# Pair sums of the late token chunks in a one-core PEER kernel: 64 candidates in place of 256

## The reference, cut to what matters

```python
s = jnp.einsum('chpd,hpnd->chpn', q, sub_keys)          # two halves p, 128 keys each
st, it = lax.top_k(s, 16)                               # best 16 of each half, in falling order
cand = st[:, :, 0, :, None] + st[:, :, 1, None, :]      # 16 x 16 = 256 pair sums
best, pos = lax.top_k(cand.reshape(...), 16)            # best 16 pairs
eidx = it_0[pos // 16] * 128 + it_1[pos % 16]           # the expert's number, of 16384
g = softmax(best)
act = gelu(u_tab[eidx] . x)                             # rows of 1024 numbers
y = sum((g * act) * v_tab[eidx])                        # rows of 1024 numbers
```

## Time and profile before

| | |
|---|---|
| median of 3 runs | 2634.97 us (2634.31 to 2636.11) |
| the profiled execution's own time | 2656.55 us |
| its span, first to last instruction | 2654.8 us |
| DVE busy | 1962.0 us (74%) |
| PE busy | 1695.6 us (64%) |
| POOL busy | 1067.3 us (40%) |
| ACT busy | 425.3 us (16%) |
| mean DMA rate over the span | 284 GB/s |

### The profile page before, as it was taken

How to read it: one execution, slowest core, us unless ns; L and a number is a source line. 1 busy time by engine, 2 the same in 40 slices (tenths; PEclk the granted TensorE clock), 3 DMA queues, 4 the chain that set the end, 5 groups by cost and what they waited for, 6 DMA issues and landing times.

```text
span 2654.8 us, 19535 instructions
## 1 busy us (share of the span) xinstructions
PE 1695.6 (64%) x5821; PEld 1073.1 (40%) x5821; DVE 1962.0 (74%) x3785; ACT 425.3 (16%) x1067; POOL 1067.3 (40%) x1028
## 2 busy tenths in 40 slices
PE   6789667989977797896000332069999998000275
PEld 2578543444336545553000322056666665000032
DVE  1331386977679778578999999988786667998844
ACT  0451201542004200111000332080000000000011
POOL 0000001325644556022544444434444445777664
PEclk9889788999988898898555555589999999555588
DMA  9657454658975798264777677859999999999997
GB/s 293 197 194 233 163 176 159 208 188 282 363 241 191 238 364 316 89 205 141 284 271 277 239 262 270 306 188 392 412 400 413 409 409 409 409 373 373 362 376 277
DMA packets 296868, 753.38 MB, mean 284 GB/s; under 512 B 21502, under 2 KB 141102, under 8 KB 296244
## 3 DMA queue, kind: packets, MB, share of 16 engines
q0 software_dynamic: 147456, 536.94, 54.7%
q1 hardware_dynamic: 149308, 215.20, 23.3%
HBM read 740.72 MB, written 11.33 MB: 283 GB/s over the span
## 4 chain that ended last, share of the span: by engine, by line
DVE 41%; issue 23%; PE 17%; DMA 10%; ACT 4%; POOL 3%; DVEq 1%; SPq 0%; ACTq 0%; another core or an unknown queue 0%; PEldq 0%; POOLq 0%; PEld 0%
DVE attn L1398 6%; PE bank L724 4%; PE pair L724 4%; DVE big L1398 4%; DVE ring_more L1398 3%; DMA ring_more<-in_peer_u_dram,eidx 3%; PE bank L973 3%; DMA attn<-in_peer_u_dram,eidx 3%; ACT work L996 2%; DMA h_all<-in_peer_v_dram,eidx 1%; PE bank L708 1%; DMA h_all<-in_peer_u_dram,eidx 1%; DMA ring_more<-in_peer_v_dram,eidx 1%; DVE work L1478 1%; PE bank L898 1%
## 5 line engine op out<-in xcount | busy, mean ns | idle before, releaser
L724 PE MATMUL pair<-big 128*128 128x128 f32 (+1 forms) x1280 | 370.6, 448 | 26.8 <-DVEq L1280 17.8
L1856 POOL DMA_INDIRECT attn<-in_peer_u_dram,eidx x225 | 224.0, 996 | 372.9 <-DVE dots L1398 241.9
L1856 POOL DMA_INDIRECT h_all<-in_peer_u_dram,eidx x106 | 119.5, 1128 | 578.1 <-DVEq L1751 420.2
L724 PE MATMUL bank<-big 128*128 128x512 f32 (+1 forms) x1056 | 315.2, 460 | 37.6 <-DVEq L1284 17.8
L1398 DVE CUSTOM_DVE_ANT_0 attn<-attn,pair 128x1024 f32<-128x1024 f32 x225 | 267.4, 1218 | 45.9 <-DMA attn<-in_peer_u_dram,eidx 36.1
L959 PE MATMUL bank<-h_all,big 128*128 128x512 f32 x608 | 271.3, 603 | 9.8 <-DMA h_all<-in_peer_v_dram 9.0
L724 PEld LDWEIGHTS pair<-big 128*128 128x128 f32 x1280 | 202.6, 200 | 182.2 <-issue 169.3
L1856 POOL DMA_INDIRECT ring_more<-in_peer_u_dram,eidx x161 | 169.8, 1054 | 197.9 <-DVE dots L1398 110.8
L724 PEld LDWEIGHTS bank<-big 128*128 128x128 f32 x1056 | 174.5, 207 | 173.6 <-issue 164.0
L959 PEld LDWEIGHTS bank<-h_all,big 128*128 128x128 f32 x608 | 180.7, 298 | 96.1 <-DMA h_all<-in_peer_v_dram 10.5
L973 PE MATMUL bank<-big,work 128*128 128x512 f32 x76 | 41.5, 686 | 278.2 <-ACT work L996 262.3
(11 more groups left out here) (261 smaller groups left out, 3129.0 us busy)
## 6 DMA issues: line engine op xcount, KB each, us to landing
big<-in_w_in_dram SPq DMA_DIRECT2D x44, 1024.0 KB, 5.7
h_all<-in_peer_v_dram SPq DMA_DIRECT2D x76, 512.0 KB
big<-in_peer_v_dram SPq DMA_DIRECT2D x52, 512.0 KB
big<-in_w_ada_dram SPq DMA_DIRECT2D x24, 1024.0 KB, 8.4
big<-in_peer_w_q_dram SPq DMA_DIRECT2D x16, 1024.0 KB, 5.5
big<-in_w_rnn_o_dram SPq DMA_DIRECT2D x8, 1024.0 KB, 8.2
big<-in_w_attn_o_dram SPq DMA_DIRECT2D x8, 1024.0 KB, 7.8
big<-in_w_out_dram SPq DMA_DIRECT2D x8, 1024.0 KB, 11.9
```

Source lines behind the costliest of these rows:

```text
L724: last = nc.tensor.matmul(u[:, 0:n], w[:, k, col:col + P], src[:, k, 0:n], start=(k == 0), stop=(k == KD - 1))
L1856: g.indirect_dma_start(dst, None, ins["peer_" + table][0], bass.IndirectOffsetOnAxis(ap=eidx[:, c, k:k + 1], axis=0)).then_inc(landed, 16)
```

## The change

For the chunks C1 + 1, C3 and C4, all routed in the late part, the 256 sums become 64, in four blocks of (i, j): i = 0 with j = 0 to 15; i = 1 to 3 with j = 0 to 7; i = 4 to 7 with j = 0 to 3; i = 8 to 15 with j = 0. They are formed for two heads at once, after every second piece. The place of a pair in the 64 is no longer 16 i + j, so a new function works i and j out, once for all 8 heads, at the start of piece 8; the two shifts, the mask and the cast in `experts` stay for chunks 0 and C1 alone. Chunks 0 and C1 are routed as before. No DMA, no PE and no ACT instruction changes.

```diff
+            def best_of_64(c, h0):
+                tv = top_v[:, c - C1, 2 * h0:2 * h0 + 4, :].rearrange("p (h s) k -> p h s k", s=2)
+                a, b = tv[:, :, 0, :], tv[:, :, 1, :]
+                s2 = cand[:, 64 * h0:64 * (h0 + 2)].rearrange("p (h n) -> p h n", h=2)
+                for lo, i0, ni, nj in ((0, 0, 1, 16), (16, 1, 3, 8), (40, 4, 4, 4), (56, 8, 8, 1)):
+                    for h in range(2):
+                        mark(V.tensor_tensor(s2[:, h, lo:lo + ni * nj].rearrange("p (i j) -> p i j", i=ni),
+                                             a[:, h, i0:i0 + ni].unsqueeze(2).to_broadcast([P, ni, nj]),
+                                             b[:, h, 0:nj].unsqueeze(1).to_broadcast([P, ni, nj]), ALU.add))
+                chain.wait()
+                for h in (h0, h0 + 1):
+                    s = cand[:, 64 * h:64 * (h + 1)]
...
+                    link(V.max(v0, s))
+                    link(V.max_index(p0, v0, s))
+                    link(V.match_replace(s, v0, s, NEG_BIG))
+                    link(V.max(v1, s))
+                    link(V.max_index(p1, v1, s))
+
+            def places_of_64():
+                i_, j_ = sel[:, 0, :], sel[:, 1, :]
+                link(V.tensor_scalar(pos[:, 1, :], pos[:, 0, :], 3, None, ALU.logical_shift_right))
+                link(V.tensor_scalar(pos[:, 2, :], pos[:, 0, :], 2, None, ALU.logical_shift_right))
+                link(V.tensor_copy(sel[:, 0:3, :], pos[:, :, :]))
+                p_, e_, q_ = sel[:, 0, :], sel[:, 1, :], sel[:, 2, :]
+                link(V.tensor_scalar(e_, e_, -1.0, 0.0, ALU.add, ALU.max))
+                link(V.scalar_tensor_tensor(e_, q_, -6.0, e_, ALU.add, ALU.max))
+                link(V.scalar_tensor_tensor(q_, p_, -48.0, e_, ALU.add, ALU.max))
+                first = sel[:, 3, :]
+                link(V.tensor_scalar(e_, q_, 8.0, 8.0, ALU.mult, ALU.add))
+                link(V.scalar_tensor_tensor(first, q_, 16.0, e_, ALU.mult, ALU.min))
+                link(V.tensor_scalar(e_, q_, 4.0, 24.0, ALU.mult, ALU.add))
+                link(V.tensor_tensor(first, first, e_, ALU.min))
+                link(V.scalar_tensor_tensor(first, q_, 48.0, first, ALU.add, ALU.min))
+                link(V.tensor_tensor(j_, p_, first, ALU.subtract))
+                link(V.tensor_copy(i_, q_))
...
-                link(V.tensor_scalar(pos[:, 1, S], pos[:, 0, S], 4, None, ALU.logical_shift_right))
-                link(V.tensor_scalar(pos[:, 2, S], pos[:, 0, S], TOPK - 1, None, ALU.bitwise_and))
-                link(V.tensor_copy(sel[:, 0:2, S], pos[:, 1:3, S]))
+                if c <= C1:
+                    link(V.tensor_scalar(pos[:, 1, S], pos[:, 0, S], 4, None, ALU.logical_shift_right))
+                    link(V.tensor_scalar(pos[:, 2, S], pos[:, 0, S], TOPK - 1, None, ALU.bitwise_and))
+                    link(V.tensor_copy(sel[:, 0:2, S], pos[:, 1:3, S]))
...
-                    best_sums(c, piece)
+                    if piece % 2:
+                        best_of_64(c, piece - 1)
                     return
                 if piece == PH:
                     best_diffs(c)
+                    places_of_64()
```

More of the change, by code:

```diff
@@ L1456, in best_sums @@
                 link(V.max_index(p1, v1, s))
+            def best_of_64(c, h0):
[10 more added lines that the diff above has]
+                    s = cand[:, 64 * h:64 * (h + 1)]
+                    v0, v1 = (best[:, 0, h * TOPK + 8 * i:h * TOPK + 8 * (i + 1)] for i in range(2))
+                    p0, p1 = (pos[:, 0, h * TOPK + 8 * i:h * TOPK + 8 * (i + 1)] for i in range(2))
+                    link(V.max(v0, s))
[3 more added lines that the diff above has]
+                    link(V.max_index(p1, v1, s))
```

## The result

| | median us | runs | ratio to before, same chip | 95% interval |
|---|---|---|---|---|
| before | 2634.58 | 6 (2628.32 to 2636.11) | | |
| changed | 2616.61 | 6 (2610.97 to 2619.21) | 0.9932 | 0.9918 to 0.9945 |
| changed, a second time (e5) | 2617.51 | 6 | 0.9939 | 0.9924 to 0.9954 |

The change makes the kernel 18.0 us faster, by the interval 14.5 to 21.6 us; 14.8 were forecast, and 2616.6 lies in the range of 2612 to 2628. The second measurement gives 0.61%, 16.1 us.

The account below looks back on a forecast made before the run. DVE's queue was taken to bound the routing of C1 + 1 and C3, full DMA engines that of C4. Per chunk 8.0 + 0.3 + 3.0 - 3.9 = 7.4 us, twice 14.8: 2634.97 - 14.8 = 2620.2 us, range 2612 to 2628.

Parts of the forecast that it names:

- DVE's queue sets the stretches A and B: Routing of C1 + 1, then of C3, before the v table: DVE full, so 2 x 7.4 = 14.8 us saved.
- searches: DVE's searches in a chunk's routing, 64 columns in place of 256 or 128: 8.0 us saved for 8 heads.
- sums: Per chunk, 32 small adds issued without a wait replace 8 adds of 256 columns: 3.7 to 3.4 us, 0.3 saved.
- the old splitting: Splitting the places in the experts' code, removed four times per chunk: 3.0 us saved.
- the new one: Working out i and j once per chunk, thirteen new DVE instructions with the cast at 0.36 us: 3.9 us added.
- DVE's waits for rows up by about 7 us: Sign in the stretch of C4's routing, where full DMA engines were to hide its 7.4 us saving.
- a shorter D would speak for the first rival: Sign: v table's first matmul to the end shorter by more than 2 us would mean C4's saving counts.
- the 10.1 us of dot products behind a piece: First stretch: 8.3 rows at 1.22 us of dot products, against 10.7 us of DMA time; delay costed at nothing.
- C4 in full: Rival: C4's routing beside the v table counts too, 22.2 us saved in all, 2612.8 us; chance 0.12.
- Adds that don't overlap: Rival: the small adds cost 6.8 us a chunk in place of 3.4; 8.0 us saved, 2627.0 us; chance 0.06.
- Gathers in DVE's place: Rival: rows come too late in 1259 to 1716 us and DVE waits; nothing gained, 2635 us; chance 0.05.
- Slower: Rival in `best_of_64`: each small add costs as much as one of 256 columns; 7.8 us lost, 2642.8; chance 0.03.

Follow-up runs that it names:

- e5: Changed kernel again, no edit; 2617.51 us, 0.9939 of before's time, first chip.
- e12: Changed kernel with one more 1024-column DVE instruction in each piece of C3's routing, 15.1 us in all; 1.0011 of before's time, first chip.
- e8: Experts of four heads at a time in place of two, on top of e7; 2608.97 us, 0.9911 of before's time, first chip.
- e2: Kernel before with only C4 routed over 64 sums, C1 + 1 and C3 as before; 1.0014 of before's time, second chip.
- e10: Kernel before with only C4 routed over 64 sums, C1 + 1 and C3 as before; 1.0010 of before's time, first chip.
- e9: Kernel before again, no edit, for a profile on the first chip; 0.9998 of before's time.
- e1: Kernel before again, no edit, for its profile, second chip; 2656.38 us, 1.0006 of before's time.
- e3: Kernel before with only C1 + 1 and C3 routed over 64 sums, C4 as before; 0.9961 of before's time, second chip.
- e4: Changed kernel with each small add waited for before the next; 0.9995 of before's time, second chip.
- e7: Changed kernel with four adds for two heads in place of eight, each twice as wide; 2615.61 us, 0.9939 of before's time, first chip.

## Why the prediction was right

**The bound.** The step that carried the forecast was that DVE's queue sets the stretches A and B, and that all behind them moves with it. e12 shows it directly for work added to B: 15.1 us make 15.3 us of B and more than 10 of the whole. For work taken away the changed kernel and e8 show it.

**The sizes.** For a chunk the terms were 8.0 + 0.3 + 3.0 - 3.9 = 7.4 us. By the rows after: searches 8 x (2 x 200 + 2 x 200 + 201 ns) = 8.0; sums 3.7 - 4 x 0.80 = 0.5; the old splitting 3.0 as put; the new one 4.04. That is 7.5, and the stretches show 7.6 to 7.9. The two terms that were off, the sums 0.2 us too small a gain and the cast some 0.1 us too cheap, partly cancel. That is luck, if a small one. The time of an add issued without a wait, for which before had no row, came out as the two copies of the earlier trace rows had said.

**The total.** By the traces on the first chip A and B together are 15.2 to 15.6 us shorter, against 14.8 forecast, and 18.0 and 16.1 measured with intervals that hold both. The 2 to 3 us between the traces' sum and the first measurement need no cause; they are less than its uncertainty.

**C4.** Costed at no gain, and e2 and e10 show none. The sign that I named for it, DVE's waits for rows up by about 7 us, is there when like stretches are compared. Over the first 225 us from the v table's first matmul such waits, on the three groups of ring tiles together, add up on the first chip to 33.8 us in before (e9), 39.7 with C4 alone changed (e10), and 43.4 and 38.3 in the two profiles of the changed kernel; on the second chip to 28.5 in before (e1), 24.5 with C4 as it was (e3) and 31.8 with C4 alone changed (e2). Two profiles of one kernel differ by up to 5 us, so this supports the 7 and doesn't measure it. The largest of the three groups (us in total, times, longest), in e9 and then in e10:

```profile
DVE attn L1398 <- DMA attn<-in_peer_u_dram,eidx: 18.3, 21, 1.3
```

```profile
DVE attn L1399 <- DMA attn<-in_peer_u_dram,eidx: 24.4, 25, 2.7
```

The same 225 us as a whole, in e9 first and then in e10: DVE is busy 6.2 us less, and the DMA engines are as full.

```profile
1783.80:2008.80 225.00, 220.23 (x506) 150.58 (x507) 185.16 (x440) 0.31 (x1) 95.53 (x102) 0.98 1.01 403
```

```profile
1792.40:2017.40 225.00, 220.31 (x506) 150.49 (x507) 178.95 (x465) 0.31 (x1) 96.69 (x102) 0.98 1.01 402
```

PE is busy 220 of the 225 us too. That the full DMA engines, and not PE's work on the v table, are what hides C4's routing is argued from the waits for rows; no run takes one of the two away, so it isn't shown.

**What stood on a wrong footing.** I made the sum against the profiled 2656.55 us and took the saving over unchanged to a median of 2634.97, without asking why one execution lies 21.6 us above three runs that agree within 2. The reason is the chip, and D, where the change saves nothing, holds nearly the whole difference; so the step was harmless here. For a change in D it would not have been. It also made one of my own signs misleading: I had written that a shorter D would speak for the first rival, and D is 21 us shorter in the changed kernel's profile than in before's. Taken at its word that sign would have called the prediction wrong, while e5 and e9, both on the first chip, have D alike. And one reading of the rows was loose: 1.22 us is how long a dot product lasts, but two start 1.14 us apart in before (at 1427.12 and 1428.26 us), so the 10.1 us of dot products behind a piece are 9.5; nothing in the sum hangs on it.

**The rivals.** C4 in full: excluded by e2 and e10. Adds that don't overlap: excluded, 0.80 us for eight. Gathers in DVE's place: waits for rows in A and B come to 0.4 us at most in any profile (e5), with none in e8, where each is 5 us shorter still. Slower: an add from start to start would have had to take 0.34 us, and takes 0.10.

**Open.** On the second chip e3 and e4 came out some 5 and 6 us worse than A and B make one expect, each by little more than its interval, and in both profiles D is 4 us longer. e2 came out 4 us above before, which is within 1 us of e10 on the first chip, with D 3 us shorter. The changed kernel itself was not run there, so its gain on that chip is not measured; e3 gained 10 us there. I don't know the cause; the DMA rate in D, which falls at times on that chip (last section), is a candidate that no run tests.

## What to carry to other kernels

Where one engine's queue is full, price a change by its instructions, and the sum comes out; where another resource is full, the same instructions were worth nothing here. Stretches between fixed events of the trace repeat to 0.4 us here and tell 1 us, where times of the whole tell 4. Cut such stretches from the events of each trace and not at the same clock times, or they hold different work. Before reading two profiles against each other, compare a stretch that the change cannot touch: if it differs beyond its own scatter, they are not from the same conditions. On DVE, small instructions that need not wait for each other should be issued together and waited for once, and wide ones save the fixed part of each.

## What the runs showed of the hardware

- Two chips run the same program 23 us apart (2632.6 and 2655.8 us, medians of 33 and 34 runs). In the profiles D holds 23.6 us of their difference, and all of that lies behind the v table: its last matmul starts at 2237.7 us in e9 and at 2239.3 in e1, of 2625.3 and 2652.2. While the v table streams beside the rows, both reach 409 GB/s (2060 to 2220). Behind it e9 keeps to 409 or 410 in each 20 us from 2260 to 2440. e1 reaches 410 as well, in four of the nine slices, and falls to as little as 284 in another; the 388 above is the mean. What makes it fall no run shows, and I have this chip from one set of runs at one time (e1 to e4), besides the profile of before. Two slices of e1:

```profile
2260.00:2280.00 20.00, 0.00 (x0) 0.00 (x0) 18.10 (x24) 0.00 (x0) 15.43 (x16) 0.50 1.03 410
...
2420.00:2440.00 20.00, 0.00 (x0) 0.00 (x0) 14.59 (x19) 0.00 (x0) 13.79 (x12) 0.50 0.84 284
```

- Adds of 8 to 24 columns: 0.10 us apart when not waited for, 0.22 us when each is.
- The cast of 384 columns took 0.47, 0.42 and 0.36 us in the routing of C1 + 1, C3 and C4, the same in two profiles to 0.01 us. The line from 64 (0.20) and 256 (0.29) columns gives 0.35; only C4's keeps to it.
- The one-hot loop (C) took 71.1 to 76.3 us with the same instructions. Its length goes with TensorE's granted clock, which stands at 0.50 (1.2 GHz) while PE has 67 us of work in 259 and rises in this loop towards 2.4 GHz. Over the loop itself the mean is 0.85 in e5 (C 71.2) and 0.74 in e10 (C 75.8) and in e7 (C 76.3), and PE is busy 43.5 us in e5 and 50.9 in e10. The loop in e5 first and then in e10:

```profile
1703.40:1774.60 71.20, 43.52 (x259) 36.69 (x259) 60.06 (x81) 57.85 (x197) 26.64 (x18) 0.85 0.59 190
```

```profile
1716.60:1792.40 75.80, 50.88 (x260) 44.37 (x260) 60.34 (x83) 58.69 (x197) 23.59 (x18) 0.74 0.56 179
```

How soon in the loop it rises was not the same in two runs of one kernel (mean 0.76 and C 74.5 in e1, 0.85 and 71.1 in e9), and accounts for up to 5 us of the scatter of the whole.
